# A hybrid attention, RWKV-7 and expert layer: the order of the recurrence's small matmuls is rewritten, and two of its groups are cut into 64x64 quarters

## The reference, cut to what matters

```python
H_R = 8; RWKV_HEAD = 64; CHUNK = 64; SEQ = 2048

def step(state, inp):                       # one token, all 8 heads, state (b, h, v, k)
    r_t, w_t, k_t, v_t, kk_t, b_t = inp
    sa = jnp.einsum('bhvk,bhk->bhv', state, -kk_t)
    state = (state * w_t[:, :, None, :] + sa[..., None] * b_t[:, :, None, :]
             + v_t[..., None] * k_t[:, :, None, :])
    return state, jnp.einsum('bhvk,bhk->bhv', state, r_t)

_, y = lax.scan(step, state0, (tm(r_h), tm(w_h), tm(k_h), tm(v_h), tm(kk), tm(b_h)))
```

## Time and profile before

| | |
|---|---|
| median of 3 runs | 3026.74 us (3025.79 to 3027.04) |
| the profiled execution | 3026.65 us, its span 3024.6 us |
| TensorE busy | 2871.2 us, 95% of the span |
| VectorE, ScalarE, GpSimd busy | 1544.2, 974.6, 643.6 us |
| mean granted TensorE clock | 0.979 of 2.4 GHz |
| the recurrence | from 1277 us to 1725 us of the span |

### The profile page before, as it was taken

One profiled execution on the slowest core, in us unless ns is written; L12 is line 12 of the kernel. 1 busy time (PEld: TensorE's weight loads), 2 busy tenths in 40 slices (PEclk: granted clock), 3 DMA queues, 4 the chain that ended last, 5 costly groups with the idle time before them and its releaser, 6 DMA issues. The chain is left out here.

```text
span 3024.6 us, 60885 instructions
## 1 busy us (share of the span) xinstructions
PE 2871.2 (95%) x22874; PEld 1816.3 (60%) x22875; DVE 1544.2 (51%) x3560; ACT 974.6 (32%) x2303; POOL 643.6 (21%) x812
## 2 busy tenths in 40 slices
PE   8999999999979999899999889994999999999999
PEld 6777878877756666688888745543333333333333
DVE  4676777767678898634344478773111111111111
ACT  3343334334447777533333324331000000000000
POOL 0000000000015555511110000111233333333333
PEclk9999999999989999999999999996999999999999
DMA  7111121111130010131111123334689779787763
GB/s 249 60 65 60 56 71 55 56 60 65 60 99 29 15 43 1 62 114 56 49 54 56 39 84 112 112 111 151 230 304 338 276 274 342 249 290 256 248 222 125
DMA packets 187585, 393.00 MB, mean 130 GB/s; under 512 B 15867, under 2 KB 74107, under 8 KB 186577
## 3 DMA queue, kind: packets, MB, share of 16 engines
q1 hardware_dynamic: 166848, 339.34, 32.7%
q0 software_dynamic: 20512, 50.54, 4.9%
HBM read 325.22 MB, written 78.22 MB: 133 GB/s over the span
## 5 line engine op out<-in xcount | busy, mean ns | idle before, releaser
L328 PE MATMUL pj_big<-pj_xnT,pj_w_in 128*128 128x256 f32 x2816 | 634.2, 381 | 2.2 <-DVE pj_xnT L467 1.5
L328 PEld LDWEIGHTS pj_big<-pj_xnT,pj_w_in 128*128 128x128 f32 x2816 | 536.8, 191 | 83.1 <-issue 5.7
L1892 PE MATMUL ex_pgu<-keep_res,ex_xT 128*64 128x512 f32 x2560 | 569.1, 597 | 0.0
L1892 PEld LDWEIGHTS ex_pgu<-keep_res,ex_xT 128*64 128x64 f32 x2560 | 177.2, 137 | 335.0 <-issue 335.0
L2000 DVE TENSOR_TENSOR ex_hh<-ex_sg,ex_pgu 128x256 f32<-128x256 f32 x80 | 33.7, 422 | 584.1 <-ACT ex_sg L1965 584.1
L1910 PE MATMUL ex_py<-keep_res,ex_hT 128*64 128x512 f32 x1280 | 288.3, 592 | 1.0 <-DVE ex_yb L2008 1.0
L767 POOL TENSOR_SCALAR at_tt<-at_e,at_cf 128x512 f32<-128x512 f32 (+3 forms) x160 | 219.3, 1373 | 177.1 <-DVE at_pd L811 164.1
L1411 PE MATMUL mg_po<-keep_res,mg_mix 128*128 128x512 f32 x512 | 233.7, 613 | 6.9 <-DVE mg_mix L1714 6.9
L298 POOL TENSOR_TENSOR pj_m<-pj_qn,pj_cosin 128x256 f32<-128x256 f32 x64 | 46.5, 727 | 823.6 <-DVE pj_qn L528 597.3
L1965 ACT ACTIVATE ex_sg<-ex_pgu 128x256 f32<-128x256 f32 x80 | 30.7, 383 | 582.2 <-PE ex_pgu L1892 582.2
L746 ACT ACTIVATE at_e<-at_sc,at_nmx 128x512 f32<-128x512 f32 (+3 forms) x320 | 196.7, 622 | 61.7 <-DVE at_nmx L789 59.3
(11 more groups left out here) (286 smaller groups left out, 4522.2 us busy)
## 6 DMA issues: line engine op xcount, KB each, us to landing
keep_res<-in_w_exp_gate SPq DMA_DIRECT2D x32, 2048.0 KB
keep_res<-in_w_exp_up SPq DMA_DIRECT2D x32, 2048.0 KB
keep_res<-in_w_exp_down SPq DMA_DIRECT2D x32, 2048.0 KB, 8.6
chunks_s<-pj_st SPq DMA_DIRECT2D x32, 642.0 KB, 4.0
rw_cin<-chunks_s SPq DMA_DIRECT2D x32, 642.0 KB, 4.1
pj_xt<-in_x SPq DMA_DIRECT2D x20, 512.0 KB, 3.7
mg_xin<-in_x SPq DMA_DIRECT2D x8, 1024.0 KB, 7.2
out<-mg_hb SPq DMA_DIRECT2D x16, 512.0 KB, 3.5
```

The costliest lines, as they stand in the source:

```text
L328: ins = pe.matmul(out, lhs, rhs, start=(k == 0), stop=(k == KC - 1))
L1892: ins = pe.matmul(pgu[j * BT:(j + 1) * BT, :, :], lhs, wgu[x][:, k, :, j * HE:(j + 1) * HE], start=(k == 0), stop=(k == KC - 1))
```

## The change

1. **Order inside groups.** `heads()` becomes `by_features()` (the same order) and `by_tokens()` (q, r, then the token half, so that the half changes with every product). `s2`, `r3q`, `r3l`, `r4` and `s0` use `by_tokens`. In `r1` and `r2`, which have two products for each head, the two halves alternate product by product.
2. **Quarters.** `gbk` is 16 products of 64x64 with 128 moving columns instead of 8 of 64x128. The part of `tok` for b and k becomes a group of its own, `bk`: 16 products of 64x64 with 64 moving columns (the identity `eye`), written to a couple laid out by head half (`keys`). `tbk` is laid out `[P, 2, NPAIR, C]` and has 3 buffers instead of 2.
3. **Order of groups.** `r5` comes ahead of `gbk`; `bk` stands behind `gbk`, and `r1` behind `bk`; v's part of `tok` is the group `v`, right behind `s3`; `r6` comes behind it.
4. **Couples.** `banks(k)` rotates the couples (`d, a, b, c` instead of `d, a, c, b`); `r1`, `r5`, `r6` and `r7` write `bc`; `bk`, `v`, `y1` and `y2` write `bb`.
5. ScalarE's order follows: `s1`, `r5`, `bk`, `r1`, `sa`, `r2`, `v`, `r3l`, `r7`, `y`. VectorE's order stays.

```diff
-PE_TURN = (("s1", 0), ("gl", 3), ("r1", 2), ("gbk", 3), ("s2", 0), ("r5", 1), ("r2", 2), ("s3", 0), ("r6", 1), ("tok", 2),
+PE_TURN = (("s1", 0), ("gl", 3), ("r5", 1), ("gbk", 3), ("bk", 2), ("r1", 2), ("s2", 0), ("r2", 2), ("s3", 0), ("v", 2), ("r6", 1),
            ("r3q", 2), ("r3l", 2), ("r7", 1), ("y1", 0), ("r4", 2), ("y2", 0), ("r8", 1), ("s0", 1))
-ACT_TURN = (("s1", 0), ("r1", 2), ("sa", 0), ("r5", 1), ("r2", 2), ("tok", 2), ("r3l", 2), ("r7", 1), ("y", 0))
+ACT_TURN = (("s1", 0), ("r5", 1), ("bk", 2), ("r1", 2), ("sa", 0), ("r2", 2), ("v", 2), ("r3l", 2), ("r7", 1), ("y", 0))
...
+        def keys(couple):
+
+            return couple.rearrange("p (r a) n -> p r (a n)", r=2)[:, :, 0:NPAIR * C]
+
+        def values(couple, rows):
+
+            return couple[rows, 1::2, 0:2 * C]
...
-                a, b, c, d = d, a, c, b
+                a, b, c, d = d, a, b, c
...
+            def by_features():
+
+                return [head(q + 2 * h, r) for q in range(2) for h in range(2) for r in range(2)]
+
+            def by_tokens():
+
+                return [head(q + 2 * h, r) for q in range(2) for r in range(2) for h in range(2)]
...
+            def b_and_k(f):
+
+                for p in range(NPAIR):
+                    for h, cols in ((0, slice(2 * C, 3 * C)), (1, slice(3 * C, 4 * C))):
                         for r in range(2):
+                            ins = f(p, r, HALVES[r], HALVES[h], cols)
...
                 if live(N_):
-                    for p, r, f, t, u, j in heads():
-                        ins = product(whole(bd)[:, r, p, :], xn[f, p, BK], xn[f, p, AR])
+                    b_and_k(lambda p, r, f, rows, cols: product(whole(bd)[rows, r, p, :], xn[f, p, cols], xn[f, p, AR]))\
+                        .then_inc(s_pe, 1)
+                if live(A_):
+                    if live(N_):
+                        pe.wait_ge(s_dve, on_dve["gl", N_])
+                    else:
+                        pe.wait_ge(s_dve, on_dve["r8", S_])
+                    b_and_k(lambda p, r, f, rows, cols: product(keys(bb)[rows, r, p * C:(p + 1) * C], xa[f, p, cols], eye[f, :]))\
+                        .then_inc(s_pe, 1)
+                    pe.wait_ge(s_dve, on_dve["gbk", A_])
+                    if live(B_):
+                        pe.wait_ge(s_act, on_act["r5", B_])
+                    l = gl[A_ % RINGS["gl"]]
+                    for q in range(2):
+                        for r in range(2):
+                            for h in range(2):
+                                p, r, f, t, u, j = head(q + 2 * h, r)
+                                product(bc[t, j, HI], l[t, j, 0, :], ga[t, r, p, LO])
+                            for h in range(2):
+                                p, r, f, t, u, j = head(q + 2 * h, r)
+                                ins = product(bc[t, j, LO], ga[t, r, p, LO], l[t, j, 0, :])
...
-                    for p in (0, 2, 1, 3):
-                        product(bc[HALVES[1 - p // 2], p, PAIR2], xa[:, p, V], ident[:, :])
-                    for p in range(NPAIR):
-                        ins = product(bc[:, p, PAIR], xa[:, p, BK], ident[:, :])
```

More of the change, by code:

```diff
@@ L848, in recur @@
         g = [old[:, n] for n in range(RINGS["g"])]
-        tbk = [m.sb(f"tbk{n}", [P, NPAIR, 2 * C]) for n in range(RINGS["tbk"])]
+        tbk = [m.sb(f"tbk{n}", [P, 2, NPAIR, C]) for n in range(RINGS["tbk"])]
         sv = [m.sb(f"sv{n}", [P, NPAIR, 2 * C]) for n in range(RINGS["sv"])]
@@ L961, in turn @@
                         pe.wait_ge(s_dve, on_dve["r8", k])
-                    for p, r, f, t, u, j in heads():
+                    for p, r, f, t, u, j in by_features():
                         ins = product(bb[t, j, LO], xn[f, p, A], xn[f, p, b_of(p)])
                     ins.then_inc(s_pe, 1)
-                if live(A_):
-                    pe.wait_ge(s_dve, on_dve["gbk", A_])
+                if live(B_):
+                    pe.wait_ge(s_dve, on_dve["r4", B_])
                     if live(k - 1):
@@ L982, in turn @@
                     pe.wait_ge(s_act, on_act["s1", S_])
[L983 removed]
+                    for p, r, f, t, u, j in by_tokens():
                         ins = product(ba[t, j, LO], q5[S_ % 2][t, j, :], sa0[t, j, :])
[L985 to L993 removed]
                     ins.then_inc(s_pe, 1)
@@ L1000, in turn @@
                     w = w2[A_ % 2]
-                    for p, r, f, t, u, j in heads():
-                        product(bd[t, j, 0:2 * C], w[t, j, 0:C], w[t, j, C:3 * C])
-                        ins = product(bd[t, j, 2 * C:3 * C], w[t, j, C:2 * C], w[t, j, 0:C])
+                    for q in range(2):
+                        for r in range(2):
+                            for h in range(2):
+                                p, r, f, t, u, j = head(q + 2 * h, r)
+                                product(bd[t, j, 0:2 * C], w[t, j, 0:C], w[t, j, C:3 * C])
+                            for h in range(2):
+                                p, r, f, t, u, j = head(q + 2 * h, r)
+                                ins = product(bd[t, j, 2 * C:3 * C], w[t, j, C:2 * C], w[t, j, 0:C])
                     ins.then_inc(s_pe, 1)
@@ L1007, in turn @@
                     pe.wait_ge(s_dve, on_dve["sa", S_])
-                    for p, r, f, t, u, j in heads():
-                        ins = product(ba[f, p, LO], tbk[S_ % RINGS["tbk"]][:, p, features(r)], sv[S_ % RINGS["sv"]][:, p, features(r)])
+                    for p, r, f, t, u, j in by_features():
+                        ins = product(ba[f, p, LO], tbk[S_ % RINGS["tbk"]][:, r, p, :], sv[S_ % RINGS["sv"]][:, p, features(r)])
+                    ins.then_inc(s_pe, 1)
+                if live(A_):
+                    for p in (0, 2, 1, 3):
+                        u = HALVES[1 - p // 2]
+                        ins = product(values(bb, u)[:, p % 2, :], xa[:, p, V], ident[:, :])
                     ins.then_inc(s_pe, 1)
@@ L1040, in turn @@
                     if live(A_):
-                        pe.wait_ge(s_act, on_act["tok", A_])
-                    elif live(k - 1):
-                        pe.wait_ge(s_act, on_act["y", k - 1])
-                    for p, r, f, t, u, j in heads():
-                        ins = product(bc[f, p, LO], state[S_ % 2][f, p, :], xs[f, p, R], first(p), False)
+                        pe.wait_ge(s_act, on_act["v", A_])
+                    for p, r, f, t, u, j in by_features():
+                        ins = product(bb[f, p, LO], state[S_ % 2][f, p, :], xs[f, p, R], first(p), False)
                     ins.then_inc(s_pe, 1)
@@ L1054, in turn @@
                     pe.wait_ge(s_pe, on_pe["y1", S_])
-                    for p, r, f, t, u, j in heads():
-                        ins = product(bc[f, p, LO], sv[S_ % RINGS["sv"]][:, p, features(r)], gs[:, r, p, HI], False, not first(p))
+                    for p, r, f, t, u, j in by_features():
+                        ins = product(bb[f, p, LO], sv[S_ % RINGS["sv"]][:, p, features(r)], gs[:, r, p, HI], False, not first(p))
                     ins.then_inc(s_pe, 1)
@@ L1091, in turn @@
                     copy("s1", S_, (sa0[:, :, :], ba[:, :, LO]))
+                if live(B_):
+                    copy("r5", B_, (ty[0][:, :, :], bc[:, :, PAIR]))
                 if live(A_):
+                    copy("bk", A_, (tbk[A_ % RINGS["tbk"]].rearrange("p r a n -> p r (a n)"), keys(bb)))
                     copy("r1", A_, (w2[A_ % 2][:, :, PAIR], bc[:, :, PAIR]))
@@ L1096, in turn @@
                                     split(ba[top, :, LO])), after="s2")
-                if live(B_):
-                    copy("r5", B_, (ty[0][:, :, :], bb[:, :, PAIR]))
                 if live(A_):
```

66 lines of the change are left out of this document (28 added, 38 removed).

## The result

| | before | after |
|---|---|---|
| median | 3026.26 us (3024.62 to 3027.04, 4 runs) | 2994.99 us (2993.76 to 2999.32, 4 runs) |
| the profiled execution | 3026.65 us | 2993.76 us |
| 29 full turns | 392.71 us, 13.54 a turn | 368.52 us, 12.71 a turn |
| TensorE idle in them with no releaser | no such row | 28.3 us |

The changed kernel takes 0.990 of the time before (0.9883 to 0.9917). It is faster, as forecast, but by 31 us and not by 65; the time lies 5 us above the upper end of the range. One execution among all those of the experiments (5590.57 us, of the version locked with `bk` late) was slow and stands in no ratio.

What follows compares the result with a forecast made beforehand. TensorE, busy 95% of the span, was taken to bound the kernel. Gains of 2.08 us a turn gave 60.3 us over 29 turns, plus 5 elsewhere: 65 us off 3026.65, so 2961 us, forecast 2950 to 2971 (chance 0.62).

Steps and rivals of the forecast that it cites:

- That 'busy' hides much: TensorE in the full turns: a matmul record lasts 218 ns, but new ones can start far closer, so starts are read.
- the four prices: TensorE records by starts: 15 ns in four quarters, 29 in two, 44 for `r1`; about 0.15 us per shape change.
- Four quarters in use: `s1` and `gl` take 15 ns a record; `gbk` in quarters with 128 columns was to take 0.90 us, not 1.09.
- The sum of 2.08 us a turn: All gains in a full turn added up: 13.51 to 11.43 us, 60.3 us over 29 turns.
- The walk through the waits: Changed turn followed from `s1`: TensorE stands 0.50 us before `r2` for ScalarE's copy of `r1`; 0.01 gained from waits.
- The first rival: In `r1` and `r2`, runs are not what slows them; 0.93 of the 2.08 us stays away: 2989 us, chance 0.12.
- The second: New waits on ScalarE and VectorE chains: two late copies cost 0.5 us a turn, 2976 us; chance 0.19 including TensorE's instructions.
- The third: Same-bank writes by the two row halves take turns: 16.0 us a turn, slower than before, 3100 us; chance 0.06.
- the fourth rival: TensorE's instruction stream limits the shorter turn: 15.1 us at the old rate, in part 0.5; chance 0.19 including new waits.
- The gain ahead of the full turns: Turn -1 should give 1 to 2 us and the turn ahead of it 1 to 3.
- The last turns: Turn 29, without `gl` and `gbk`, was to take some 1.1 us less than 11.42; the last two change little.

Runs made afterwards that it cites:

- the version locked with `bk` late: Changed kernel with `gbk` as 8 products, turns padded to 768 instructions, and `bk` moved between `s2` and `r2`: 0.987 of the kernel before.
- the kernel with the twos alone: Kernel before, with only the two products of a head in `r1` and `r2` alternating between the halves: 0.9916 of the kernel before, 12.74 us a turn.
- the supply run: Kernel before plus 512 products of 64x64 in all four quarters (2048 instructions) ahead of the first turn: 3053.72 us, the added stretch 38.8 us.
- the lock: Changed kernel with `gbk` as 8 products and five semaphore increments a turn from k = 4, making 768 instructions: 0.9838 of the kernel before, 11.85 us a turn.
- `gbk` whole: Changed kernel with `gbk` again as 8 products of 64 rows by 128 columns, 32 instructions fewer a turn: 0.9852 of the kernel before, 12.20 us a turn.

## Why the prediction was wrong

**The reading of the turn was right.** "That 'busy' hides much", and the four prices from the earlier trace rows, held to within 0.06 us in every group, for the new ones too. "Four quarters in use" with 128 moving columns, which no row showed, took 0.88 for 0.90. The sum of 2.08 us a turn is what the shortest turns show: 11.39 for 11.43.

**The walk through the waits was right in size.** TensorE waits before `r2` and nowhere new. In turn k = 6, `r1`'s last record begins at 1382.25 and `r2` at 1383.26, 1.01 us later; the walk had 1.00 (3.28 to 4.28). In most turns `r2` begins 0.44 us behind the last record of `s2`, where the walk's 0.50 us of standing and one step of 0.03 make 0.53. The wait view shows only 5.5 us in all for ScalarE's copies, 0.2 a turn, since it counts from the end of that last record, which lasts 0.22.

**The first rival fell.** `r1` takes 0.93 and `r2` 1.49; the kernel with the twos alone says the same. **The second** had no place in the traces: no wait of TensorE's products for ScalarE or VectorE exceeds 0.2 us but one of 0.6 at ScalarE's copy of `sv`. **The third fell entirely.** Groups whose row halves write the same bank one right after the other (`r3q`, `r3l`) take 0.47 us, the full rate of two quarters; the price it would have needed was 0.93. The Trainium skill's rule (TensorEngine Tiling (Array Packing), Gotcha 1: PSUM Pressure) that row tiles can't access one bank simultaneously showed no cost here, where they write different partitions.

**The step that failed is the fourth rival's.** It was the right mechanism, "TensorE's instructions", and it was weighed down by one sentence: "now too, `r3q` to `y1`'s end has 80 records in 1.98 us, 40 a us". These 80 records are 160 instructions, less than one block of 256. A burst shorter than a block says nothing about the rate at which blocks come. To test it, one has to look over several blocks, and the trace of before had the numbers: 81 blocks in 392.71 us, 4.85 us each. At the forecast 11.43 us a turn, 795 instructions would have needed a block every 3.68 us as a mean. Single blocks of before took as little as 3.39 us, but no two in a row less than 3.92 on average: such a rate, held from block to block, the recurrence had nowhere shown. Before, the supply had slack nearly everywhere; even so its turn -1 had a stop of 0.51 us with no releaser.

The price was off too. I allowed it "0.5 us a turn"; it was 1.28 in the profiled execution. The measured turn is 12.71 us for 3.1 blocks, 4.09 us a block, while the supply run got one every 3.46 with the DMA engines idle, and the full turns of the kernel after have none under 3.42. The rest is unevenness: a four-quarter group starts 32 records in 0.47 us, so 256 instructions of that kind go in 1.9 us, while a block of `r2`, `s3` and `v` lasts much longer. Whether the slow part of one block makes up for the fast part of the next depends on where the boundary lies, and 795 instructions move it by 27 from turn to turn. This fits that one turn has 11.39 and another 13.38 us; I haven't worked it out turn by turn.

**The other terms.** The gain ahead of the full turns was 5.8 us, a little above the bounds. The last turns gave nothing where 1.1 us was forecast; why is not shown (the versions with the twos alone and with the lock had their turn 29 at 10.7 us, the kernel after at 11.47).

**What stays open.** How far ahead a block is asked for, and so which place of the boundary is best, was not worked out for any version. Nor is it known what fills the 1.2 to 1.6 us between the end of a block's packet and TensorE's next product. The two profiled executions of the kernel after differ by 0.3 us a turn, and I have no cause for that.

## What to carry to other kernels

Count the instructions (a float32 product is four, seen as two matmuls and two weight loads) of a stage with many small products, divide by 256, and compare the time that a block has left with what blocks are seen to take here: 3.4 to 3.5 us at the least with the DMA engines idle or lightly loaded, 6.2 us with them full, and some 4 us as the mean of the turns of the kernel after, whose groups are of uneven density. Below that a faster group mostly turns into idle time without a releaser, and the edits that pay are those that add no instruction (the order in twos: 0.8 us a turn) or remove some (`gbk` whole: more time by the clock, yet faster in all). When a loop runs near the limit, its length in instructions is a parameter of its own: in a turn that is a whole number of blocks the blocks end at the same places each time, and these may be good or bad ones (2970.7 and 2989.77 us for the same turns). Padding costs time too where nothing covers it: an increment takes 0.15 us.

## What the hardware showed that I had not expected

- TensorE ran 128 records of matmuls with their 128 weight loads and stood for the next 256 instructions, with nothing else to wait for: 2 to 3 us each time with the DMA engines at 1.03 of their time, a block every 6.2 us; with them at 0.02 a block came every 3.46 us.
- All 228 stops with no releaser, in 14 traces, lie at one remainder of the instruction count by 256.
- Five semaphore increments on TensorE took 0.15 us each; uncovered, they moved the next group from 0.05 to 0.63 us behind the last record.
- A product with 4 moving columns takes as long as one with 64: 29 ns a record with two quarters in use, 58 in its own quarter. With 128 columns, four quarters together, 32 records took 0.88 us, 110 ns a record in its quarter.
- Thirty products ahead of a loop made the loop 20 us longer (363.54 against 343.52), by moving the places where its instruction blocks end.
